# Sums of squares from the untransposed input, and the first two units of a layer with their high-part passes ahead

## The chip, the cores and the metric

The kernel runs on one core of a Trainium2 chip. The metric is the device time of one execution in microseconds. TensorE, VectorE, ScalarE and GpSimd (POOL in the profile) run their own instruction streams and wait for each other by semaphores; SyncE (SP) issues most of the DMAs.

## What is computed

The reference is a trunk of two layers over 512 tokens of width 1024, all in float32. Cut to what matters here:

```python
def rms_norm(x, g, eps=NORM_EPS):
    x32 = x.astype(F32)
    y = x32 * lax.rsqrt(jnp.mean(x32 * x32, axis=-1, keepdims=True) + eps)
    return (y * g.astype(F32)).astype(x.dtype)

for l in range(DEPTH):
    h = rms_norm(x, mix_norm_g[l])
    p_gdn, p_mla, p_rwkv, p_dsa, p_gate = _split(h @ w_in[l], SLAB_SPLITS)
    ...
    x = x + merged @ w_o[l]
    hm = rms_norm(x, mlp_norm_g[l])
    x = x + jnp.square(jax.nn.relu(hm @ w_up[l])) @ w_down[l]
return rms_norm(x, final_norm_g)
```

## The kernel before, in words

Activations are kept transposed: xT holds x as 8 tiles of 128 features by 512 tokens. The input x arrives with tokens on the partitions (`xin`, 4 tiles of 128 tokens by 1024 features, in two DMAs that each bring 512 feature columns). TensorE transposes it, one bank of 128x512 for each of the 8 feature tiles (L741, four transposes each), and VectorE copies each bank into xT (L1539).

The weights come as a stream of units; each is 1024x128 (8 blocks of 128x128, 512 KB) and goes to a ring of 3 slots. For each unit ScalarE rounds the weights to their high part (`split_next`, L1070, `w_hi`), GpSimd subtracts it to get the low part (L428, two halves, `w_lo`). The two `w_hi`/`w_lo` slots are used in turn. ScalarE's queue holds `split_next` at fixed places: units 0 and 1 at its start, each later unit just after the bank of the unit two earlier has been taken. A product of a unit with the activations is three passes of 8 matmuls into one bank (`feat_group`, `split_product`): high weights by high activations (L467) and high weights by low activations (L468) in turn, tile by tile, then low weights by high activations (L471). The pools of banks are `bank_a` (3 banks, emptied by ScalarE) and `bank_v` (4 banks, emptied by VectorE).

The norm ahead of a layer: for each tile of xT ScalarE squares it (L1078, `square`), VectorE adds it to a running 128x512 sum (L1388, `add_square`). Then TensorE sums that over the partitions with 4 matmuls against a column of ones (L494, `token_root`), which puts the sum of each token on the token's own partition: 128x4. VectorE scales it and takes the reciprocal (L1394, L1396), ScalarE the square root (L1082), and TensorE spreads it over the partitions with 4 matmuls (L500). VectorE then multiplies each tile of xT by the gain and the root (L1402, `mg`), ScalarE rounds it to its high part (L1086, `h_hi`), and VectorE subtracts to get the low part (L1406, `h_lo`). In `norm` VectorE's order is: product of tile k, then low part of tile k-1. The first unit of a layer, `("rw", 0)`, waits on TensorE for the low part of tile k before its two matmuls of that tile. It and the following ones (`project_rw(4)`) are taken from their banks by ScalarE (L1142, `take_rw`), each followed by the split of the next unit.

In layer 0 alone, VectorE computes arguments of rotary tables right after the norm (L1552 to L1568). ScalarE's queue holds two pairs of sines for them (L1134, L1135) after `h_hi` and before the first `take_rw`, with a wait for VectorE's arguments ahead of each.

Of the kernel before, what the change touches and what calls it, by code (L numbers as in the profile page):

```python
# [25 lines left out]
L = 2  # L26
# [134 lines left out]
def build(nc, x_in, pos_in, wstream, par_in, const_in, tabs, x_dram, out):  # L161
    ctx = ExitStack()
    with ctx:
# [117 lines left out]
        def at(l, name, k):  # L281

            return l * per[key[name]] + before[name] + k
# [164 lines left out]
        def _(pe):  # L448
# [38 lines left out]

            def token_root(l):

                b, reader, emptied = banks.next("v", "n_var")  # L490
                pe.wait_ge(reader, emptied)
                pe.wait_ge(S["n_acc"], at(l, "n_acc", 7))
                for t in range(TT):
                    ins = mm(b[:, t:t + 1], sums[0][:, t * P:(t + 1) * P], cst("ones")[:, 0:1], start=True, stop=True)  # L494
                ins.then_inc(v_full, 1)
                b, reader, emptied = banks.next("v", "n_g", at(l, "n_g", KT))
                pe.wait_ge(reader, emptied)
                pe.wait_ge(S["n_rs"], at(l, "n_rs", 1))
                for t in range(TT):
                    ins = mm(b[:, t * P:(t + 1) * P], root[:, t:t + 1].to_broadcast([P, P]), cst("ident"), start=True, stop=True)  # L500
                ins.then_inc(v_full, 1)
# [241 lines left out]

            for l in range(L):
                token_root(l)
                if l == 0:
# [4 lines left out]
                def project_rw(count):  # L751
                    for _ in range(count):
                        i = next(rw)
                        if i == 0:
                            feat_group(("rw", i), l, h_hi, h_lo, "a", "r_in", "n_h", at(l, "n_h", 0))
                        else:
                            feat_group(("rw", i), l, h_hi, h_lo, "a", "r_in")

# [5 lines left out]

                project_rw(4)

# [188 lines left out]
                for q in range(QUARTERS + 1):  # L955
# [7 lines left out]
                    if q >= 1:  # L963
                        for i in range(8):
# [3 lines left out]
                            else:  # L968
                                feat_group(("down", q - 1, i), l, hi, lo, "v", "down_done")
            token_root(L)  # L970
            for half in range(2):
# [11 lines left out]
        def _(act):  # L983
# [133 lines left out]
            def sums_done(name, n):  # L1117

                sums_counts[name] = sums_counts.get(name, 0) + n
                return sums_counts[name]  # L1120

            split_next()
            split_next()
            for l in range(L):
                if l == 0:
                    for k in range(KT):
                        act.wait_ge(S["x_t"], k + 1)
                        square(0, 0, k)
                norm_root(l)
# [225 lines left out]
        def _(dve):  # L1355
# [35 lines left out]
            def norm(l, gain, parts=True):  # L1391
                dve.wait_ge(v_full, filled.next())
                b = filled.bank()
                v.tensor_scalar(root, b[:, 0:TT], 1.0 / D, EPS, MUL, ADD).then_inc(S["n_var"], 1)  # L1394
                dve.wait_ge(S["n_var"], reached("n_var"))
# [3 lines left out]
                b = filled.bank()  # L1399
                for k in range(KT + 1):  # L1400
                    if k < KT:
                        ins = v.scalar_tensor_tensor(mg[:, k, :], xT[:, k, :], pr(gain, k), b[:], MUL, MUL)  # L1402
                        ins.then_inc(S["n_g"], 1)
                    if parts and k >= 1:
                        dve.wait_ge(S["n_hi"], at(l, "n_hi", k))
                        v.tensor_tensor(h_lo[:, k - 1, :], mg[:, k - 1, :], h_hi[:, k - 1, :].bitcast(F32), SUB).then_inc(S["n_h"], 1)  # L1406

# [128 lines left out]
            for k in range(KT):  # L1536
# [3 lines left out]
                dve.wait_ge(S["x_t"], reached("x_t"))  # L1540
                if k:
                    add_square(0, 0, k - 1)
            add_square(0, 0, KT - 1)

# [437 lines left out]
```

## Time and profile before

| | us |
|---|---|
| median of 3 runs | 2219.42 |
| lowest and highest run | 2217.23, 2220.02 |
| profiled execution, its time | 2219.2 |
| its span, first to last instruction | 2217.4 |
| TensorE matmul busy | 2110.0 (95%) |
| VectorE busy | 1133.7 (51%) |
| ScalarE busy | 751.1 (34%) |
| GpSimd busy | 738.3 (33%) |
| mean granted TensorE clock | 0.978 |

The profile is of one execution. Busy time of TensorE is modelled and overlaps from one matmul to the next; the distance between two starts says more. The granted clock is given as a share of 2.4 GHz. The idle time of an engine stands in brackets behind an instruction, with what ended it.

### The profile page before, as it was taken

What the parts mean: (1) busy time and instruction counts of PE and PEld (TensorE: products, weight loads), DVE (VectorE), ACT (ScalarE), POOL (GpSimd) and SP (SyncE); (2) the same over time, 40 slices, a digit from 0 to 9 for tenths busy, and PEclk for the clock granted to TensorE, in tenths of its full rate; (3) what the DMA queues carried; (4) which work ended last, traced back from release to release, by engine and by line L of the source; (5) the groups of instructions that cost most, each with busy time, mean ns of one, the idle gap of its engine ahead of it and who ended that gap; (6) DMA issues with size and microseconds to landing.
All of it is one profiled execution on the core that took longest, in us unless ns stands there. A gap on an engine that the chain in (4) does not pass through costs nothing.

```text
span 2217.4 us, 34596 instructions
## 1 busy us (share of the span) xinstructions
PE 2110.0 (95%) x14488; PEld 1630.3 (74%) x14488; DVE 1133.7 (51%) x1894; ACT 751.1 (34%) x1136; POOL 738.3 (33%) x550
## 2 busy tenths in 40 slices
PE   4999999998999999999989999999899999999997
PEld 3778787765666888888867877876565678888886
DVE  5785654897373422222256854569855534222223
ACT  3541513323342342322244253133243433322312
POOL 1540312321223444444435122133122244444442
PEclk7999999999999999999989999999899999999998
DMA  4320111221311332332232111022112123333321
GB/s 163 103 86 17 46 31 58 88 69 39 107 46 62 103 97 94 100 93 96 93 104 88 48 35 54 31 74 79 60 58 86 38 84 95 95 96 95 97 93 67
DMA packets 52266, 170.03 MB, mean 77 GB/s; under 512 B 5648, under 2 KB 13968, under 8 KB 51600
## 3 DMA queue, kind: packets, MB, share of 16 engines
q1 hardware_dynamic: 50928, 162.75, 22.8%
q0 software_dynamic: 1184, 5.07, 0.6%
q8 instruction: 116, 1.90, 0.4%
q14 instruction: 38, 0.31, 0.0%
HBM read 160.45 MB, written 7.34 MB: 76 GB/s over the span
## 4 chain that ended last, share of the span: by engine, by line
PE 77%; DVE 18%; ACT 3%; issue 2%; DMA 1%; SPq 0%; DVEq 0%; ACTq 0%
PE bank_a L467 11%; PE bank_a L468 11%; PE bank_a L471 10%; PE bank_v L471 7%; PE bank_v L467 7%; PE bank_v L468 7%; PE bank_v L607 5%; PE bank_v L529 3%; DVE arena L1776 3%; DVE m L1774 2%; PE bank_v L723 2%; PE bank_v L705 1%; DVE arena L1372 1%; DVE mg L1378 1%; DVE arena L1767 1%
## 5 line engine op out<-in xcount | busy, mean ns | idle before, releaser
L428 POOL TENSOR_TENSOR w_lo<-ring,w_hi 128x512 fp32r<-128x512 f32 x536 | 731.8, 1386 | 1309.7 <-ACT w_hi L1070 1309.6
L467 PE MATMUL bank_a<-h_hi,w_hi 128*128 128x512 f32 x1376 | 561.2, 408 | 8.2 <-DVE h_lo L1406 4.8
L468 PE MATMUL bank_a<-h_lo,w_hi 128*128 128x512 f32 x1376 | 540.9, 393 | 0.0
L1070 ACT ACTIVATE w_hi<-ring 128x1024 fp32r<-128x1024 f32 x268 | 281.6, 1051 | 234.5 <-DVE arena L1881 220.2
L471 PE MATMUL bank_a<-h_hi,w_lo 128*128 128x512 f32 x1376 | 340.0, 389 | 0.0
L467 PEld LDWEIGHTS bank_a<-h_hi,w_hi 128*128 128x128 f32 x1376 | 260.7, 189 | 86.4 <-issue 18.8
L468 PEld LDWEIGHTS bank_a<-h_lo,w_hi 128*128 128x128 f32 x1376 | 261.5, 190 | 60.9 <-issue 8.7
L471 PEld LDWEIGHTS bank_a<-h_hi,w_lo 128*128 128x128 f32 x1376 | 258.4, 188 | 53.9
L1372 DVE TENSOR_TENSOR sg<-bank_v,sg 128x512 f32<-128x512 f32 x112 | 77.5, 692 | 349.4 <-PE bank_v L471 256.5
L467 PE MATMUL bank_v<-parts,w_hi 128*128 128x512 f32 x640 | 254.4, 398 | 1.4 <-DVE parts L1852 1.4
L468 PE MATMUL bank_v<-parts,w_hi 128*128 128x512 f32 x640 | 253.4, 396 | 0.0
L1871 DVE TENSOR_TENSOR arena<-arena 128x512 f32<-128x512 f32 x64 | 44.3, 692 | 245.2 <-ACT arena L1336 245.1
L471 PE MATMUL bank_v<-parts,w_lo 128*128 128x512 f32 x640 | 162.2, 395 | 0.0
L467 PEld LDWEIGHTS bank_v<-parts,w_hi 128*128 128x128 f32 x640 | 120.3, 188 | 32.7 <-DVE parts L1852 4.0
L468 PEld LDWEIGHTS bank_v<-parts,w_hi 128*128 128x128 f32 x640 | 120.1, 188 | 29.5 <-issue 0.5
L471 PEld LDWEIGHTS bank_v<-parts,w_lo 128*128 128x128 f32 x640 | 120.2, 188 | 29.1
L607 PE MATMUL bank_v<-arena 64*64 64x64 f32 x3712 | 112.1, 219 | 5.9 <-DVE arena L1447 5.0
L607 PEld LDWEIGHTS bank_v<-arena 64*64 64x64 f32 x3712 | 110.7, 135 | 7.0 <-DVE arena L1447 5.7
L529 PE MATMUL bank_v<-yo,out_ring 128*128 128x512 f32 x256 | 114.0, 592 | 0.0
L1336 ACT ACTIVATE arena<-bank_a 128x512 f32<-128x512 f32 x64 | 38.3, 598 | 205.6 <-PE bank_a L471 205.6
L1372 DVE TENSOR_TENSOR arena<-arena 128x512 f32<-128x512 f32 (+5 forms) x80 | 88.1, 1102 | 37.7 <-ACT arena L1142 29.4
L1040 ACT ACTIVATE sg<-bank_a 128x512 f32<-128x512 f32 x56 | 33.4, 597 | 212.4 <-PE bank_a L471 212.4
(267 smaller groups left out, 2441.7 us busy)
## 6 DMA issues: line engine op xcount, KB each, us to landing
ring<-in_w SPq DMA_DIRECT2D x268, 512.0 KB, 3.5
out_ring<-in_w SPq DMA_DIRECT2D x64, 128.0 KB, 3.5
x_dram<-arena SPq DMA_DIRECT2D x2, 2048.0 KB, 7.6
arena<-x_dram SPq DMA_DIRECT2D x2, 2048.0 KB, 8.1
arena<-in_x SPq DMA_DIRECT2D x2, 1024.0 KB, 8.6
arena<-tabs POOLq DMA_DIRECT2D x4, 512.0 KB, 4.0
out_x<-arena SPq DMA_DIRECT2D x2, 1024.0 KB, 4.4
par<-in_par POOLq DMA_DIRECT2D x2, 937.0 KB, 7.0
```

Source lines behind the costliest of these rows:

```text
L428: ins = nc.gpsimd.tensor_tensor(w_lo[:, g % SPLIT, ks, :], raw, w_hi[:, g % SPLIT, ks, :].bitcast(F32), ALU.subtract)
L467: mm(b[:], w_hi[:, s, k, :], hi[:, k, :], start=k == 0, stop=False)
L468: mm(b[:], w_hi[:, s, k, :], lo[:, k, :], start=False, stop=False)
L471: ins = mm(b[:], w_lo[:, s, k, :], hi[:, k, :], start=False, stop=k == KT - 1)
L529: ins = mm(b[:], out_ring[:, n % OUT_RING, k, :], yo[:, slot, k, :], start=k == 0, stop=k == 1)
L607: ins = mm(b[quarter(p_), k * C:(k + 1) * C], lhs[quarter(p_), m, :], rhs(m, p_), start=True, stop=True)
L723: ins = mm(b[rows, 0:P], v[:, k, h * C:(h + 1) * C], V_pt(x)[:, j % 2, k, :], start=k == 0, stop=k == qt)
L1070: act_fn(w_hi[:, g % SPLIT, :, :], ring[:, g % RING, :, :], ACT.Copy).then_inc(S["split_hi"], 1)
L1372: link(v.tensor_tensor(out_, a, b, op))
L1774: link(v.max(m8[:], src))
L1776: link(v.match_replace(wk, m8[:], src, -3e38))
L1871: v.tensor_tensor(relu2[:, n % 2, :], relu[:, n % 2, :], relu[:, n % 2, :], MUL).then_inc(S["up_sq"], 1)
```

## The change

Three things are changed. In layer 0, ScalarE squares `xin` itself, 8 pieces of 128 tokens by 512 features, with a sum along the row (`accum_out`) into 8 columns of `att`; it does so before the splits of units 0 and 1. VectorE adds the two halves (128x4) into `root`. The squares of xT, their sums and the 4 matmuls of L494 are gone in layer 0; in layer 1 and in the final norm they stay (`token_sums`). In `norm`, VectorE issues all 8 products and then all 8 low parts. On TensorE, `project_first` takes the place of the first two of `project_rw(4)`, in both layers: for unit 0 and then unit 1, tile by tile, high by high and low weights by high activations; then the 8 low-activation matmuls of unit 0, then those of unit 1.

```diff
@@ -485,7 +485,7 @@
                 pe.wait_ge(S["n_acc"], at(l, "n_acc", 14))
                 mm(b[:], cst("ones"), sums[1], start=True, stop=True).then_inc(v_full, 1)
 
-            def token_root(l):
+            def token_sums(l):
 
                 b, reader, emptied = banks.next("v", "n_var")
                 pe.wait_ge(reader, emptied)
@@ -493,6 +493,9 @@
                 for t in range(TT):
                     ins = mm(b[:, t:t + 1], sums[0][:, t * P:(t + 1) * P], cst("ones")[:, 0:1], start=True, stop=True)
                 ins.then_inc(v_full, 1)
+
+            def token_root(l):
+
                 b, reader, emptied = banks.next("v", "n_g", at(l, "n_g", KT))
                 pe.wait_ge(reader, emptied)
                 pe.wait_ge(S["n_rs"], at(l, "n_rs", 1))
@@ -742,6 +745,10 @@
                 ins.then_inc(v_full, 1)
 
             for l in range(L):
+                if l == 0:
+                    banks.counts["n_var"] = 1
+                else:
+                    token_sums(l)
                 token_root(l)
                 if l == 0:
                     pe.wait_ge(more_here, 16)
@@ -750,11 +757,26 @@
 
                 def project_rw(count):
                     for _ in range(count):
-                        i = next(rw)
-                        if i == 0:
-                            feat_group(("rw", i), l, h_hi, h_lo, "a", "r_in", "n_h", at(l, "n_h", 0))
-                        else:
-                            feat_group(("rw", i), l, h_hi, h_lo, "a", "r_in")
+                        feat_group(("rw", next(rw)), l, h_hi, h_lo, "a", "r_in")
+
+                def project_first():
+
+                    open_ = []
+                    for _ in range(2):
+                        g = begin_unit(("rw", next(rw)), l)
+                        b, reader, emptied = banks.next("a", "r_in")
+                        pe.wait_ge(reader, emptied)
+                        pe.wait_ge(S["split_lo"], g + 1)
+                        open_.append((g % SPLIT, b))
+                        for k in range(KT):
+                            pe.wait_ge(S["n_hi"], at(l, "n_hi", k + 1))
+                            mm(b[:], w_hi[:, g % SPLIT, k, :], h_hi[:, k, :], start=k == 0, stop=False)
+                            mm(b[:], w_lo[:, g % SPLIT, k, :], h_hi[:, k, :], start=False, stop=False)
+                    for s, b in open_:
+                        for k in range(KT):
+                            pe.wait_ge(S["n_h"], at(l, "n_h", k + 1))
+                            ins = mm(b[:], w_hi[:, s, k, :], h_lo[:, k, :], start=False, stop=k == KT - 1)
+                        ins.then_inc(a_full, 1)
 
                 def low_rank(weights, act_tile):
                     for f in range(2):
@@ -762,7 +784,8 @@
                         pe.wait_ge(reader, emptied)
                         mm(b[:], weights[:, f * P:(f + 1) * P], act_tile, start=True, stop=True).then_inc(a_full, 1)
 
-                project_rw(4)
+                project_first()
+                project_rw(2)
 
                 pe.wait_ge(S["r_act"], at(l, "r_act", 1))
                 low_rank(pr("wa2")[0:64, :], R["rm"][0:64, 6, :])
@@ -967,6 +990,7 @@
                                 feat_group(("down", q - 1, i), l, hi, lo, "v", "down_done", "up_done", at(l, "up_done", 8 * (q - 1)))
                             else:
                                 feat_group(("down", q - 1, i), l, hi, lo, "v", "down_done")
+            token_sums(L)
             token_root(L)
             for half in range(2):
                 for t in range(TT):
@@ -1119,13 +1143,14 @@
                 sums_counts[name] = sums_counts.get(name, 0) + n
                 return sums_counts[name]
 
+            for half in range(2):
+                act.wait_ge(x_here[half], 16)
+                for t in range(TT):
+                    act_fn(ar(8 + TT * half + t, (T,)), xin[:, t, half * T:(half + 1) * T], ACT.Square,
+                           accum_out=att[:, half, t:t + 1]).then_inc(S["n_sq"], 1)
             split_next()
             split_next()
             for l in range(L):
-                if l == 0:
-                    for k in range(KT):
-                        act.wait_ge(S["x_t"], k + 1)
-                        square(0, 0, k)
                 norm_root(l)
                 if l == 0:
 
@@ -1389,21 +1414,21 @@
                     dve.wait_ge(S["n_acc"], reached("n_acc"))
 
             def norm(l, gain, parts=True):
-                dve.wait_ge(v_full, filled.next())
-                b = filled.bank()
-                v.tensor_scalar(root, b[:, 0:TT], 1.0 / D, EPS, MUL, ADD).then_inc(S["n_var"], 1)
+                token_sum = root
+                if l:
+                    dve.wait_ge(v_full, filled.next())
+                    token_sum = filled.bank()[:, 0:TT]
+                v.tensor_scalar(root, token_sum, 1.0 / D, EPS, MUL, ADD).then_inc(S["n_var"], 1)
                 dve.wait_ge(S["n_var"], reached("n_var"))
                 v.reciprocal(root, root).then_inc(S["n_rec"], 1)
                 dve.wait_ge(S["n_rec"], reached("n_rec"))
                 dve.wait_ge(v_full, filled.next())
                 b = filled.bank()
-                for k in range(KT + 1):
-                    if k < KT:
-                        ins = v.scalar_tensor_tensor(mg[:, k, :], xT[:, k, :], pr(gain, k), b[:], MUL, MUL)
-                        ins.then_inc(S["n_g"], 1)
-                    if parts and k >= 1:
-                        dve.wait_ge(S["n_hi"], at(l, "n_hi", k))
-                        v.tensor_tensor(h_lo[:, k - 1, :], mg[:, k - 1, :], h_hi[:, k - 1, :].bitcast(F32), SUB).then_inc(S["n_h"], 1)
+                for k in range(KT):
+                    v.scalar_tensor_tensor(mg[:, k, :], xT[:, k, :], pr(gain, k), b[:], MUL, MUL).then_inc(S["n_g"], 1)
+                for k in range(KT if parts else 0):
+                    dve.wait_ge(S["n_hi"], at(l, "n_hi", k + 1))
+                    v.tensor_tensor(h_lo[:, k, :], mg[:, k, :], h_hi[:, k, :].bitcast(F32), SUB).then_inc(S["n_h"], 1)
 
             def low_part(l, k):
 
@@ -1538,9 +1563,10 @@
                 b = filled.bank()
                 v.tensor_copy(xT[:, k, :], b[:]).then_inc(S["x_t"], 1)
                 dve.wait_ge(S["x_t"], reached("x_t"))
-                if k:
-                    add_square(0, 0, k - 1)
-            add_square(0, 0, KT - 1)
+            dve.wait_ge(S["n_sq"], 8)
+            v.tensor_tensor(root, att[:, 0, :], att[:, 1, :], ADD).then_inc(S["n_acc"], 7)
+            counts["n_acc"] = 7
+            dve.wait_ge(S["n_acc"], 7)
 
             for l in range(L):
                 dve.wait_ge(par_here, 16 * (l + 1))
```

ScalarE's queue at the start, before. L1078 are the squares of xT, L1082 the root:

```order
L1070 ACT_TABLE_LOAD
L1070 ACTIVATE w_hi<-ring 128x1024 x2
L1078 ACTIVATE arena<-arena 128x512 x8
L1082 ACT_TABLE_LOAD
L1082 ACTIVATE sml<-sml 128x4
L1086 ACTIVATE h_hi<-mg 128x512 x8
```

And with the change, where L1149 are the squares of `xin`, L1094 the splits and L1106 the root:

```order
L1149 ACT_TABLE_LOAD
L1149 ACTIVATE arena,att<-arena 128x512 x8
L1094 ACTIVATE w_hi<-ring 128x1024 x2
L1106 ACT_TABLE_LOAD
L1106 ACTIVATE sml<-sml 128x4
L1110 ACTIVATE h_hi<-mg 128x512 x8
```

The squares moved ahead of the two splits, and nothing but a table load now stands between splits and root.

VectorE in the start and norm of layer 0, before (the pair of L1402 and L1406 goes on to 8 each):

```order
L1539 COPY arena<-bank_v3 128x512
L1388 TENSOR_TENSOR arena<-arena 128x512 x2
L1394 TENSOR_SCALAR sml<-bank_v0 128x4
L1396 RECIPROCAL sml<-sml 128x4
L1402 SCALAR_TENSOR_TENSOR mg<-arena,par,bank_v1 128x512 x2
L1406 TENSOR_TENSOR h_lo<-mg,h_hi 128x512
L1402 SCALAR_TENSOR_TENSOR mg<-arena,par,bank_v1 128x512
```

And with the change:

```order
L1564 COPY arena<-bank_v3 128x512
L1567 TENSOR_TENSOR sml<-att 128x4
L1421 TENSOR_SCALAR sml<-sml 128x4
L1423 RECIPROCAL sml<-sml 128x4
L1428 SCALAR_TENSOR_TENSOR mg<-arena,par,bank_v0 128x512 x8
L1431 TENSOR_TENSOR h_lo<-mg,h_hi 128x512 x8
L1578 CAST arena<-arena 128x512
```

The large sums (L1388) are gone, and products and low parts stand in two blocks ahead of the tables' first instruction.

TensorE in the first two units, before:

```order
L500 MATMUL bank_v1<-consts,sml 128x128 x4
L467 MATMUL bank_a0<-h_hi,w_hi 128x512
L468 MATMUL bank_a0<-h_lo,w_hi 128x512
...
L471 MATMUL bank_a0<-h_hi,w_lo 128x512 x8
L467 MATMUL bank_a1<-h_hi,w_hi 128x512
```

And with the change:

```order
L503 MATMUL bank_v0<-consts,sml 128x128 x4
L773 MATMUL bank_a0<-h_hi,w_hi 128x512
L774 MATMUL bank_a0<-h_hi,w_lo 128x512
...
L773 MATMUL bank_a1<-h_hi,w_hi 128x512
L774 MATMUL bank_a1<-h_hi,w_lo 128x512
...
L778 MATMUL bank_a0<-h_lo,w_hi 128x512 x8
L778 MATMUL bank_a1<-h_lo,w_hi 128x512 x8
```

All 16 matmuls that read low activations moved behind the 32 that read high ones; unit 0's bank is complete 8 matmuls before unit 1's.

## Rows read from the trace of the kernel before

**Rows 1.** The page, chain that ended last, by engine.

```profile
PE 77%; DVE 18%; ACT 3%; issue 2%; DMA 1%; SPq 0%; DVEq 0%; ACTq 0%
```

**Rows 2.** Timeline, start of layer 0: start us, us, engine, line, operation [idle before].

```profile
8.69 4.57 PE L741 MATMUL bank_v<-consts,arena 128*128 128x128 f32 x24 [8.69 <-DMA arena<-in_x]
9.91 1.51 DVE L1539 COPY arena<-bank_v 128x512 f32<-128x512 f32 x2 [7.32 <-PE bank_v L741]
16.11 1.06 ACT L1070 ACTIVATE w_hi<-ring 128x1024 fp32r<-128x1024 f32 x1 [14.09 <-DMA ring<-in_w]
17.25 5.39 POOL L428 TENSOR_TENSOR w_lo<-ring,w_hi 128x512 fp32r<-128x512 f32 x4 [15.30 <-ACT w_hi L1070]
17.39 1.06 ACT L1070 ACTIVATE w_hi<-ring 128x1024 fp32r<-128x1024 f32 x1 [0.22 <-DMA ring<-in_w]
...
19.05 0.69 DVE L1539 COPY arena<-bank_v 128x512 f32<-128x512 f32 x1 [7.63 <-ACT arena L1078]
...
28.95 1.28 ACT L1082 ACT_TABLE_LOAD   x1
...
32.26 0.20 ACT L1082 ACTIVATE sml<-sml 128x4 f32<-128x4 f32 x1 [2.03 <-DVE sml L1396]
...
34.77 1.41 DVE L1402 SCALAR_TENSOR_TENSOR mg<-arena,par,bank_v 128x512 f32<-128x512 f32 x2 [2.54 <-PE bank_v L500]
```

**Rows 3.** Timeline of the norm in layer 0, and last line the final norm.

```profile
39.34 0.74 DVE L1402 SCALAR_TENSOR_TENSOR mg<-arena,par,bank_v 128x512 f32<-128x512 f32 x1
...
40.11 0.63 ACT L1086 ACTIVATE h_hi<-mg 128x512 fp32r<-128x512 f32 x1 [0.63 <-DVE mg L1402]
40.60 0.74 DVE L1402 SCALAR_TENSOR_TENSOR mg<-arena,par,bank_v 128x512 f32<-128x512 f32 x1
...
44.55 0.69 DVE L1406 TENSOR_TENSOR h_lo<-mg,h_hi 128x512 fp32r<-128x512 f32 x1
...
2202.88 5.36 DVE L1402 SCALAR_TENSOR_TENSOR mg<-arena,par,bank_v 128x512 f32<-128x512 f32 x8 [2.54 <-PE bank_v L500]
```

**Rows 4.** Timeline, the sine that waits in layer 0 and unit 2's first matmul.

```profile
53.78 0.63 ACT L1134 ACTIVATE arena<-arena 128x512 f32<-128x512 f32 x1 [2.93 <-DVE arena L1562]
...
56.42 0.59 PE L467 MATMUL bank_a<-h_hi,w_hi 128*128 128x512 f32 x1 [2.56 <-ACT w_hi L1070]
```

**Rows 5.** Timeline, layer 1: the norm's start, units 0 and 1 taken.

```profile
1120.70 1.41 DVE L1402 SCALAR_TENSOR_TENSOR mg<-arena,par,bank_v 128x512 f32<-128x512 f32 x2 [2.54 <-PE bank_v L500]
...
1134.18 0.60 ACT L1142 ACTIVATE arena<-bank_a 128x512 f32<-128x512 f32 x1 [3.73 <-PE bank_a L471]
...
1139.62 0.60 ACT L1142 ACTIVATE arena<-bank_a 128x512 f32<-128x512 f32 x1 [3.89 <-PE bank_a L471]
```

**Rows 6.** Windows: stretch, us, busy PE, PEld, DVE, ACT, POOL, granted clock, DMA share, GB/s.

```profile
37.00:46.00 9.00, 8.76 (x16) 4.12 (x17) 8.87 (x15) 5.07 (x7) 0.00 (x0) 0.50 0.00 0
...
56.40:60.00 3.60, 3.58 (x9) 2.84 (x10) 3.50 (x3) 1.40 (x2) 3.56 (x3) 0.54 0.00 0
1122.00:1131.00 9.00, 7.82 (x13) 3.51 (x14) 8.87 (x15) 4.52 (x8) 0.00 (x0) 0.50 0.58 245
```

**Rows 7.** Groups by line with shapes: an ACTIVATE that sums along the row.

```profile
L1095 ACT ACTIVATION_READ_ACCUMULATOR arena<-arena,att 128x1 f32 x64 | 12.0, 187 | 0.0
...
L1095 ACT ACTIVATE arena<-arena,att 128x512 f32<-128x512 f32 x16 | 11.6, 723 | 21.3 <-DVE att L1512 21.3
```

**Rows 8.** Timeline, a table load and the ACTIVATE behind it.

```profile
65.33 1.28 ACT L1159 ACT_TABLE_LOAD   x1
...
66.62 0.63 ACT L1159 ACTIVATE arena<-arena 64x512 f32<-64x512 f32 x1
```

**Rows 9.** Timeline, matmuls in unit 2 of layer 0, and 8 at full clock.

```profile
57.66 0.63 PE L468 MATMUL bank_a<-h_lo,w_hi 128*128 128x512 f32 x1
...
58.08 0.63 PE L467 MATMUL bank_a<-h_hi,w_hi 128*128 128x512 f32 x1
...
1137.61 1.98 PE L471 MATMUL bank_a<-h_hi,w_lo 128*128 128x512 f32 x8
```

## The prediction

> **What bounds the kernel now.** I read three views in this order. First the chain that ended last: TensorE is 77% of it, VectorE 18% [rows 1]. So time is won only where TensorE stands still or runs at its lower clock while others work, and the change touches two such places: the start of each layer. Then the timeline: the first 57 us [rows 2, 3, 4], the same place in layer 1 [rows 5]. Last the granted clock by stretch [rows 6].
>
> At the start of layer 0 TensorE transposes x from 8.69. VectorE empties two banks, and its next copy begins at 19.05, with 7.63 us of waiting for ScalarE's first square [rows 2]. ScalarE stood in its queue at the two weight splits, which waited for DMA until 16.11 and 17.39 and end at 17.39 + 1.06 = 18.45. Only then do the squares and their sums start, alternating between ScalarE and VectorE until the table load at 28.95. The gain multiplication, which I call the norm's start S, comes at 34.77 [rows 2].
>
> After S each of the 8 tiles costs 1.26 us (39.34 to 40.60), because VectorE alternates product and low part and the product waits behind the low part of the tile before [rows 3]. The last low part ends at 44.55 + 0.69 = 45.24, that is S + 10.47. TensorE follows tile by tile and is granted 0.50 of full speed, the 1.2 GHz level, all through it [rows 6]. VectorE then computes arguments of the rotary tables. ScalarE waits for them with the first unit's bank and the split of unit 2 behind them in its queue. So unit 2's first matmul is at 56.42, after 2.56 us in which TensorE had nothing to do [rows 4]. Layer 1 has no tables there: unit 0 is taken at 1134.18 and unit 1 at 1139.62, so unit 1 was done about 18.9 us after its S of 1120.70 [rows 5].
>
> **The change, part by part.**
>
> *Squares from x as it arrives.* Removed: 8 squares and 7 VectorE sums, 4 matmuls (L494) in layer 0. Added: 8 squares on ScalarE that also sum along the row, and one 128x4 addition. Such an ACTIVATE of 128x512 takes 723 ns and its READ_ACCUMULATOR 187 ns [rows 7], so 0.91 us each. Four may start when the first half of x is there (8.69), until 12.3. The second half was there before TensorE ended its 24 transposes at 13.26 [rows 2], since six column tiles need it. Four more end between 16.0 and 16.9. The two splits stand behind them, but could not start before 16.11 anyway, and the second not before 17.39. So they end at 18.45 or up to 0.5 later. I take 18.5.
>
> VectorE now copies eight banks back to back: 1.51 us for two [rows 2], so 9.91 + 8 x 0.75 = 15.9. The addition and two small operations end before 16.7, or 17.6 with late squares. So the root waits only for ScalarE: 18.5, table load 1.28 = 19.8, root 0.20 = 20.0. From the root's end (32.26 + 0.20 = 32.46) to S it took 2.31 us [rows 2]. New S: 22.3, that is **12.5 us earlier** (12.0 to 12.5).
>
> The load's price is weighed here. A load of 1.28 us at 65.33 is followed by its ACTIVATE at 66.62 [rows 8], so nothing more than the load is on the path. The Trainium skill, page "ScalarE: Activation LUTs", section "What ACT_TABLE_LOAD costs", adds about 1.38 us of drain to every switch, 2.66 us together. By the page S would be 23.7 and the gain of this part 11.1; [rows 8] decide, and the sum goes by them.
>
> *POOL's queue and DMA.* GpSimd makes the low parts of units 0 and 1 from 17.25 to 22.64 [rows 2]. Unit 0 is ready halfway, at 20.0, before the new S, and unit 1 at 22.6, long before TensorE asks. The copy of xT to DRAM is issued some 5 us earlier, behind the same two ring loads; nobody waits for it until much later. Cost nothing.
>
> *VectorE's order within the norm.* Eight products back to back took 5.36 us in the final norm [rows 3], 0.66 apart. The eight low parts follow at 0.62 to 0.73 apart (a row of 0.69, less an overlap like that of the products, or with a step between them). The last ends at S + 10.2 to 11.1, and I take S + 10.5, as before. So the rotary tables start as before relative to S and **unit 2 still starts 21.65 us after S**: about 44.0 in place of 56.42. In layer 0 the new order of units 0 and 1 gains nothing, for TensorE will be done by about 38 and then idles some 6 us. That wait hides the whole of it. Were the tables gone, it would be worth what layer 1 shows.
>
> *Low clock behind that wait.* After the wait of 2.56 us the granted clock is 0.54 from 56.4 to 60.0 [rows 6]. Matmuls were 0.42 us apart there (57.66, 58.08), against (1.98 - 0.39) / 7 = 0.227 at full clock [rows 9]. Eight matmuls cost 8 x 0.19 = 1.6 us more. A longer wait leads to the same half clock. I take the same 1.6 us, so 0 change. Bounds: 1.6 gained if the clock is back at once, 2.6 lost if it takes the 9 us that the paced start took.
>
> *TensorE's order, layer 1.* The high part of tile k is ready at S + 0.77 + 0.63 + 0.66 k [rows 3], so TensorE starts at S + 1.45 and no longer waits for low parts. It has 16 + 16 high-part matmuls, then 8 + 8 low-part ones. Before, 16 matmuls were spread over 10 us. Now two per tile take 0.85 us at the lower clock against a supply of 0.66, so TensorE is fed without gaps. The open size is when the clock rises. As nearest rows, the unbroken unit 2 of layer 0 had it back 3.6 us after its first matmul; the paced starts had 0.50 for 9 us [rows 6].
> - Back after 3.6 us: 8.5 matmuls by S + 5.1. The supply then paces until S + 6.5, and the other 32 take 32 x 0.227 = 7.3: end S + 13.8, gain 5.1.
> - Back after 9 us: 21 matmuls by S + 10.5, 27 more in 6.1: end S + 16.6, gain 2.3.
>
> I take 5 us, nearer to the unbroken row: 11.8 matmuls by S + 6.5, 36.2 x 0.227 = 8.2, end S + 14.7, **gain 4.2**. Low parts are in time: the last is at S + 10.5, needed after S + 12. Unit 2's split is now behind unit 0's late end: taking the bank and splitting are 0.5 + 1.05 us, and unit 0 ends 8 matmuls = 1.8 us before unit 1. So this new wait stays covered, by 0.2 us.
>
> *Final norm*: same work. **Sum**: 12.5 - 0.1 + 4.2 = 16.6, of which I keep 16.4 for small handovers. The profiled execution took 2219.2 (span 2217.4), so 2202.8; the median of the runs is 0.2 higher, so **2203.0 us**.
>
> **The rivals.**
> 1. *The clock gives less.* Layer 1 keeps 0.50 for 9 us, and the longer wait before unit 2 costs 2.6 more: 12.4 + 2.3 - 2.6 = 12.1, 2207. For it: [rows 6], two paced starts of 9 us. Against it: these had gaps, the new one has none.
> 2. *ScalarE's queue moves late.* Each us by which the squares end after 16.1 pushes both splits, root and S. For a gain below 10.5 they would need 0.7 us more each than the rows of such squares show [rows 7]. Also a piece of the 12.4 could vanish in a later wait for another engine. Some 6 us of gain left: 2213.
> 3. *The change does not do what it says*: the norm's start in layer 0 still waits for an input that I see as landed, and the layer 1 order is worth nothing as unit 2's split is late: 2218.
> 4. *Slower: the half clock spreads.* Place: layer 0, from the new wait before unit 2 on, and layer 1's first units. Each us of unbroken matmuls at 1.2 GHz costs 1 - 0.227/0.42 = 0.46 us. To lose 16.4 and another 4.4 (0.2%), 45 us more at 0.50 are needed. The trace shows 9 us at most in one piece [rows 6]. If all 48 matmuls of both first pairs stayed low, layer 1 would end at S + 1.45 + 20.2 = 21.6, 2.7 us later than before, still far from it. From 45 us on it decides: 2224.
>
> **How the numbers follow.** 0.2% of this time, 4.4 us, is about what a measurement of this kernel can tell from no change. Forecast 0.71 (its own range 2199 to 2206: 5.1 in place of 4.2, a clock 1.6 better, and the same down). Rival 1 has 0.17, rival 2 0.07, rival 3 0.03, rival 4 0.02. Forecast, rival 1 and rival 2 are faster by more than 4.4: 0.95, less 0.01 for rival 2's tail. Rival 3 and that tail are the same: 0.04. Slower 0.02. The range 2198.5 to 2209 holds the forecast and rival 1 with its bound.
>
> **What would show it.** In the new profile: eight copies without a gap until 16, splits at 16.1 and 17.4, gain products from 22.3, table arguments from 33, unit 2's first matmul at 44.0 with 5 to 7 us of idle time before it, released by the split; in layer 1 matmuls from S + 1.45 without gaps and unit 1 taken at S + 14.7, last low part at S + 10.5. Wrong are the steps where S falls later than 23, where unit 2 begins later than 45.5, or where layer 1's unit 1 is taken after S + 17. A span that moves less than these three together would speak for a later wait.

## The result and the profile after

The changed kernel took 2201.57 us (median of 4 runs, 2198.79 to 2202.93) against 2219.18 (4 runs, 2217.23 to 2220.02): ratio 0.992, 95% interval 0.9903 to 0.9937, 17.6 us less. The profiled execution took 2201.45 us with a span of 2199.7.

Where the 17.7 us of the span came from, at five places of the two timelines:

| place | before | after | earlier by |
|---|---|---|---|
| S, layer 0 | 34.77 | 22.32 | 12.45 |
| unit 2's first matmul, layer 0 | 56.42 | 43.68 | 12.74 |
| S, layer 1 | 1120.70 | 1108.98 | 11.72 |
| unit 1 taken, layer 1 | 1139.62 | 1123.44 | 16.18 |
| S, final norm | 2202.88 | 2185.13 | 17.75 |

The timeline of the changed kernel at the start answers to [rows 2]. Columns: start us, us, engine, line, operation, [idle before]:

```profile
8.76 0.63 ACT L1149 ACTIVATE arena<-arena 128x512 f32<-128x512 f32 x1 [6.73 <-DMA arena<-in_x]
...
13.89 0.19 ACT L1149 ACTIVATION_READ_ACCUMULATOR arena<-arena 128x1 f32 x1
...
16.16 1.06 ACT L1094 ACTIVATE w_hi<-ring 128x1024 fp32r<-128x1024 f32 x1 [2.09 <-DMA ring<-in_w]
...
17.44 1.06 ACT L1094 ACTIVATE w_hi<-ring 128x1024 fp32r<-128x1024 f32 x1 [0.22 <-DMA ring<-in_w]
18.52 1.28 ACT L1106 ACT_TABLE_LOAD   x1
19.81 0.21 ACT L1106 ACTIVATE sml<-sml 128x4 f32<-128x4 f32 x1
20.16 2.05 PE L503 MATMUL bank_v<-consts,sml 128*128 128x128 f32 x8 [6.25 <-ACT sml L1106]
22.32 5.36 DVE L1428 SCALAR_TENSOR_TENSOR mg<-arena,par,bank_v 128x512 f32<-128x512 f32 x8 [5.61 <-PE bank_v L503]
```

The eight squares run from 8.76 to 14.08 and are over 2 us before the first split can start. The root follows the table load at once. TensorE's start and unit 2, which answer to [rows 3, 4]:

```profile
23.88 0.77 PE L773 MATMUL bank_a<-h_hi,w_hi 128*128 128x512 f32 x1 [1.67 <-ACT h_hi L1110]
...
27.59 4.91 DVE L1431 TENSOR_TENSOR h_lo<-mg,h_hi 128x512 fp32r<-128x512 f32 x8
...
33.51 3.79 PE L778 MATMUL bank_a<-h_lo,w_hi 128*128 128x512 f32 x16
...
43.68 0.80 PE L467 MATMUL bank_a<-h_hi,w_hi 128*128 128x512 f32 x1 [6.38 <-ACT w_hi L1094]
```

TensorE has done both units at 37.3 and then waits 6.38 us for the split behind the sines; before it was 2.56. The windows view, with the columns of [rows 6], shows what follows:

```profile
23.80:28.40 4.60, 4.52 (x11) 3.60 (x12) 4.60 (x8) 4.43 (x8) 0.00 (x0) 0.50 0.93 364
28.40:37.30 8.90, 8.90 (x39) 6.99 (x37) 8.62 (x16) 1.58 (x2) 0.00 (x0) 0.98 0.23 96
37.30:43.60 6.30, 0.00 (x1) 0.00 (x0) 5.81 (x12) 3.37 (x7) 0.00 (x0) 0.90 0.01 1
43.60:49.00 5.40, 5.32 (x13) 4.17 (x14) 5.24 (x5) 1.46 (x3) 5.30 (x4) 0.50 0.25 66
1110.50:1114.00 3.50, 3.46 (x8) 2.80 (x9) 3.50 (x6) 3.37 (x6) 0.00 (x0) 0.50 1.03 430
1114.00:1121.00 7.00, 7.00 (x32) 5.70 (x31) 5.34 (x11) 0.99 (x2) 0.00 (x0) 0.99 0.25 105
```

Fed without gaps, TensorE was at full clock 4.9 us after its first matmul in layer 0 and 3.6 us after it in layer 1, where the paced starts of [rows 6] had 0.50 for 9 us. But behind the long wait it had 0.50 from 43.6 to 49.0, which is why 12.74 us shrank to 11.75 when unit 2's bank was taken (63.77 before, 52.02 after). In layer 1, answering to [rows 5]:

```profile
1121.62 0.60 ACT L1167 ACTIVATE arena<-bank_a 128x512 f32<-128x512 f32 x1 [6.61 <-PE bank_a L778]
...
1123.44 0.60 ACT L1167 ACTIVATE arena<-bank_a 128x512 f32<-128x512 f32 x1 [0.27 <-PE bank_a L778]
```

Unit 1 is taken 14.46 us after S, where it was 18.92.

### The profile page after: what moved, and what is told of

It reads as the page before. It is cut to its first block, busy times and chain, and to the rows that moved or that the text cites. A ratio compares the mean times of both kernels' runs of the same rounds, so it can differ in the third digit from the quotient of the medians.

```text
span 2199.7 us, 34572 instructions
## 1 busy us (share of the span) xinstructions
PE 2100.2 (95%) x14480; PEld 1627.7 (74%) x14480; DVE 1127.3 (51%) x1888; ACT 752.1 (34%) x1144; POOL 739.9 (34%) x550
## 4 chain that ended last, share of the span: by engine, by line
PE 77%; DVE 18%; ACT 3%; issue 1%; DMA 1%; SPq 0%; DVEq 0%; ACTq 0%
PE bank_a L467 11%; PE bank_a L468 10%; PE bank_a L471 10%; PE bank_v L471 7%; PE bank_v L467 7%; PE bank_v L468 7%; PE bank_v L610 5%; PE bank_v L532 3%; DVE arena L1802 3%; DVE m L1800 3%; PE bank_v L726 2%; PE bank_v L708 1%; DVE arena L1397 1%; DVE mg L1403 1%; DVE arena L1793 1%
## 5 line engine op out<-in xcount | busy, mean ns | idle before, releaser
L467 PE MATMUL bank_a<-h_hi,w_hi 128*128 128x512 f32 x1344 | 543.5, 404 | 6.8 <-ACT w_hi L1094 6.8
L468 PE MATMUL bank_a<-h_lo,w_hi 128*128 128x512 f32 x1344 | 525.3, 391 | 0.0
L1094 ACT ACTIVATE w_hi<-ring 128x1024 fp32r<-128x1024 f32 x268 | 281.7, 1051 | 222.4 <-DVE arena L1907 220.1
L471 PE MATMUL bank_a<-h_hi,w_lo 128*128 128x512 f32 x1344 | 332.0, 389 | 0.0
L467 PEld LDWEIGHTS bank_a<-h_hi,w_hi 128*128 128x128 f32 x1344 | 253.5, 189 | 75.1 <-issue 13.5
L468 PEld LDWEIGHTS bank_a<-h_lo,w_hi 128*128 128x128 f32 x1344 | 253.6, 189 | 60.4 <-issue 8.7
L471 PEld LDWEIGHTS bank_a<-h_hi,w_lo 128*128 128x128 f32 x1344 | 252.3, 188 | 52.4
```

The lines of the kernel that those rows point to most:

```text
L467: mm(b[:], w_hi[:, s, k, :], hi[:, k, :], start=k == 0, stop=False)
L468: mm(b[:], w_hi[:, s, k, :], lo[:, k, :], start=False, stop=False)
L471: ins = mm(b[:], w_lo[:, s, k, :], hi[:, k, :], start=False, stop=k == KT - 1)
L1094: act_fn(w_hi[:, g % SPLIT, :, :], ring[:, g % RING, :, :], ACT.Copy).then_inc(S["split_hi"], 1)
```

## The experiments

Eleven kernels ran, each timed against the kernel before on the same chip. The median of the kernel before was 2218.59 us beside e1 to e4, 2218.89 beside e5, e6, e7 and e9, and 2218.66 beside e10 to e12. S, "unit 2" and "unit 1 taken" are the places of the table above; all line numbers in rows are those of the kernel named.

### Taking the change apart

**e1_squares**: the early squares alone.

```diff
-                project_first()
-                project_rw(2)
+                project_rw(4)
...
-                for k in range(KT):
-                    v.scalar_tensor_tensor(mg[:, k, :], xT[:, k, :], pr(gain, k), b[:], MUL, MUL).then_inc(S["n_g"], 1)
-                for k in range(KT if parts else 0):
+                for k in range(KT + 1):
```

> Only the squares from the untransposed x; norm order and TensorE's order of units 0 and 1 as before. Theory (the early start is worth 12.4 us in layer 0, and the new order is worth nothing there because the rotary tables hold unit 2 back; it is worth 4.5 us in layer 1 alone): S of layer 0 at 22.3, unit 2's first matmul at 43.7 to 44.0, layer 1's unit 1 taken at its S + 18.9, total 2206.5 us. Rival (the order gives 4 us in both layers): unit 2 only at 47.5 and total about 2210. Either may be off by 1.6 us for each piece of 3.4 us at the lower clock more or less.

Measured: 2205.93 us (2205.05 to 2206.22), ratio 0.9943 (0.9926 to 0.9959). S at 22.45, unit 2 at 44.12, unit 1 of layer 1 taken at S + 19.00. The theory held and the rival, with unit 2 at 47.5, falls.

**e2_order**: both new orders, the squares as before. The diff is against the kernel before; those of the other runs are against the changed kernel.

```diff
-                project_rw(4)
+                project_first()
+                project_rw(2)
...
-                for k in range(KT + 1):
...
+                for k in range(KT):
+                    v.scalar_tensor_tensor(mg[:, k, :], xT[:, k, :], pr(gain, k), b[:], MUL, MUL).then_inc(S["n_g"], 1)
+                for k in range(KT if parts else 0):
```

> Only the new orders on VectorE and TensorE, in both layers; the squares as before. Theory: unit 2 of layer 0 at 56.4 as before, since it is released by ScalarE after the tables; unit 1 of layer 1 at S + 14.5 in place of 18.9; total 2214.7 us. Rival (the order gives 4 us in both layers): unit 2 at 52.5, total 2210.

Measured: 2213.39 us (10 runs, 2211.34 to 2217.09), ratio 0.9977 (0.9968 to 0.9987). Unit 2 at 56.15, after a wait of 6.97 us; unit 1 of layer 1 taken at S + 14.12. So the early squares are worth 12.7 us and the orders 5.2, and 17.9 is the whole change within the spread. In layer 0 the orders did not move unit 2 (56.42 to 56.15).

**e3_pe_old** and **e4_alt**: the changed kernel with one of the two orders put back.

```diff
-                project_first()
-                project_rw(2)
+                project_rw(4)
```

> The changed kernel with TensorE's old order of units 0 and 1; VectorE's eight products stay ahead of the eight low parts. Theory (the gain of layer 1 needs both orders): the first matmul waits for the first low part, at S + 6.0 in place of S + 1.5, then unit 1 ends at about S + 18.6, as before the change; total 2206 us. Rival (VectorE's order alone does it): S + 15, total 2201.6.

```diff
-                for k in range(KT):
-                    v.scalar_tensor_tensor(mg[:, k, :], xT[:, k, :], pr(gain, k), b[:], MUL, MUL).then_inc(S["n_g"], 1)
-                for k in range(KT if parts else 0):
+                for k in range(KT + 1):
```

> The changed kernel with VectorE's old order, product and low part in turn; TensorE's new order stays. Theory: high parts come 1.26 us apart, so the high passes of unit 0 last until S + 10.5 with gaps, the clock stays at 0.50 until about then, and unit 1 ends at S + 18 to 19.5; total 2206 us. Rival (TensorE's order alone does it): S + 15, total 2201.6.

Measured: 2205.21 us (2202.98 to 2205.87) and 2203.81 (2202.49 to 2207.24). Layer 1's unit 1 was taken at S + 19.62 and S + 18.46. Both rivals fall: against the S + 19.00 of e1_squares, one order without the other is 0.6 us later or 0.5 earlier in layer 1, where both together are 4.5 earlier. The timeline of e3_pe_old shows the new wait that VectorE's blocks make for TensorE's old order:

```profile
1105.20 5.36 DVE L1431 SCALAR_TENSOR_TENSOR mg<-arena,par,bank_v 128x512 f32<-128x512 f32 x8 [2.54 <-PE bank_v L503]
1110.47 4.90 DVE L1434 TENSOR_TENSOR h_lo<-mg,h_hi 128x512 fp32r<-128x512 f32 x8
...
1111.31 0.77 PE L467 MATMUL bank_a<-h_hi,w_hi 128*128 128x512 f32 x1 [6.21 <-DVE h_lo L1434]
```

One number was not expected: e3_pe_old has its S of layer 1 at 1105.20, where the changed kernel has 1108.98. In layer 0 its unit 2 began at 43.84 after a wait of only 1.46 us, and its bank was taken at 49.62, in the changed kernel at 52.02. That raised a question that the prediction had not: does TensorE's new order cost something in layer 0?

### What the place of the squares and of the root is worth

**e9_late**: the squares behind the two splits.

```diff
+            split_next()
+            split_next()
             for half in range(2):
                 act.wait_ge(x_here[half], 16)
...
-            split_next()
-            split_next()
```

> The changed kernel with the eight squares behind the two weight splits on ScalarE. Theory: squares from 18.5, 0.62 us apart as in the changed kernel's trace, until 23.5, S at 27.3 in place of 22.3, unit 2 at 48.7, total 2206.6 us. Rival (the place of the squares does not matter, as the splits and DMA set S): S at 22.5, total 2201.6.

Measured: 2205.8 us (2203.7 to 2207.38). S at 27.33 and unit 2 at 48.68, 5.0 us later than in the changed kernel; the median is 4.2 above. The rival falls. S is still 7.4 us earlier than in the kernel before, so of the 12.45 us the place in the queue gave 5.0. The other 7.4 came with the squares of `xin` themselves, which need no turns with VectorE's copies and sums and no matmuls of L494.

**e7_root**: the root ahead of the splits, its inputs computed between two of VectorE's copies.

```diff
                 act_fn(root, root, ACT.Sqrt).then_inc(S["n_rs"], 1)
+                if l == 0:
+                    split_next()
+                    split_next()
...
-            split_next()
-            split_next()
...
             for k in range(KT):
+                if k == 6:
+                    dve.wait_ge(S["n_sq"], 8)
+                    v.tensor_tensor(root, att[:, 0, :], att[:, 1, :], ADD).then_inc(S["n_acc"], 7)
...
                 v.tensor_copy(xT[:, k, :], b[:]).then_inc(S["x_t"], 1)
```

> The changed kernel, with the root of layer 0 ahead of the two weight splits on ScalarE, and the addition and reciprocal between VectorE's sixth and seventh copy. Theory (the splits, which wait for the weights' DMA, and the table load behind them set S): S at 17.9 in place of 22.3, unit 2 at 39.3, total 2197.2 us. Rival (the norm now runs beside GpSimd's low parts, 17.3 to 22.6, and its products are slowed): S at 17.9 but the last low part less than 2 us earlier than in the changed kernel, total 2200.

Measured: 2195.18 us (2194.64 to 2195.92), ratio 0.9894 (0.9879 to 0.9909), 6.4 below the changed kernel. Its timeline:

```profile
15.23 0.20 ACT L1106 ACTIVATE sml<-sml 128x4 f32<-128x4 f32 x1
...
15.58 1.13 PE L503 MATMUL bank_v<-consts,sml 128*128 128x128 f32 x8 [1.52 <-ACT sml L1106]
16.01 1.06 ACT L1094 ACTIVATE w_hi<-ring 128x1024 fp32r<-128x1024 f32 x1 [0.58 <-DMA ring<-in_w]
16.85 5.36 DVE L1427 SCALAR_TENSOR_TENSOR mg<-arena,par,bank_v 128x512 f32<-128x512 f32 x8 [0.71 <-PE bank_v L503]
17.16 5.00 POOL L428 TENSOR_TENSOR w_lo<-ring,w_hi 128x512 fp32r<-128x512 f32 x4 [15.19 <-ACT w_hi L1094]
```

S is 5.47 us earlier and unit 2 5.48 (38.20). I had expected 4.4: TensorE's spreading matmuls (L503) take 1.13 us in place of 2.05, for they come 1.52 us behind the transposes and have a granted clock of 1.00 (15.5 to 16.8), where in the changed kernel they come after 6.25 us and have 0.50 (20.1 to 22.3). The eight products beside GpSimd's low parts take 5.36 us, as without them, and the last low part of the norm ends 5.5 us earlier, so that rival falls.

### Whether the tables are the whole bound of layer 0

**e5_tables**: ScalarE takes units 0 and 1, and splits units 2 and 3, ahead of the sines.

```diff
-                if l == 0:
-
-                    for i in range(2):
-                        act.wait_ge(S["tab_arg"], i + 1)
...
-                for i in range(3):
-                    take_rw(i)
+                take_rw(0)
+                take_rw(1)
+                if l == 0:
+
+                    for i in range(2):
+                        act.wait_ge(S["tab_arg"], i + 1)
...
+                take_rw(2)
```

> The changed kernel, with ScalarE taking units 0 and 1 and splitting units 2 and 3 ahead of the sines in layer 0. Theory (the tables alone hold unit 2 back, and the low clock behind the wait is a cost of that wait): unit 2's first matmul at about 37.5 in place of 43.7 with almost no idle time, no fall of the clock there, 8.8 us less up to there; some of it given back before the low-rank matmuls, since VectorE still has the tables to do, slowed while GpSimd splits units 2 and 3: total 2194.5 us (2192 to 2197). Rival (VectorE is the bound of that stage whatever ScalarE does): all given back at the low-rank matmuls, total 2200 to 2202.

Measured: 2201.86 us (2201.52 to 2202.58). The rival's total was right: all was given back, though not where it had said.

```profile
34.18 2.14 DVE L1404 SCALAR_TENSOR_TENSOR arena<-arena 128x512 f32<-128x512 f32 x3
...
37.65 6.12 POOL L428 TENSOR_TENSOR w_lo<-ring,w_hi 128x512 fp32r<-128x512 f32 x4 [15.55 <-ACT w_hi L1094]
39.26 5.06 DVE L1404 SCALAR_TENSOR_TENSOR arena<-arena 128x512 f32<-128x512 f32 x3
...
48.33 3.33 DVE L1607 SCALAR_TENSOR_TENSOR arena<-arena,par 128x512 f32<-128x512 f32 x1
...
51.73 1.28 ACT L1185 ACT_TABLE_LOAD   x1 [4.33 <-DVE arena L1607]
...
53.71 6.20 PE L785 MATMUL bank_a<-arena,par 64*128 64x512 f32 x8 [4.92 <-ACT arena L1185]
```

TensorE went on to unit 2 at 37.6, but the low-rank matmuls (L785) wait 4.92 us for ScalarE, and that 4.33 us for VectorE. VectorE was busy for 28.5 of the 29.4 us from S on: three operations of the second table took 5.06 us beside GpSimd's splits, where the first table's took 2.14, and the operation that ScalarE waits for (L1607) took 3.33 us, the next one like it 0.75. So VectorE's work is the bound up to there, not only the place of the split in ScalarE's queue. Yet the low-rank matmuls still begin 3.65 us earlier than in the changed kernel (57.36). The rest was given back behind them, by the clock. First e5_tables, then the changed kernel:

```profile
53.80:64.00 10.20, 10.20 (x18) 5.39 (x19) 8.48 (x20) 5.75 (x8) 3.09 (x2) 0.50 0.19 59
```

```profile
57.30:64.00 6.70, 6.40 (x23) 3.91 (x23) 5.66 (x7) 4.13 (x7) 3.12 (x2) 1.00 0.37 101
```

Behind its 4.92 us of waiting e5_tables has half clock for 10.2 us, some 4.7 us lost at the prediction's 0.46 for each (an estimate). At layer 1's S it is 1.66 us behind the changed kernel (1110.64).

**e6_tables_pe_old**: the same with TensorE's old order.

```diff
-                project_first()
-                project_rw(2)
+                project_rw(4)
```

> As the run with the sines moved behind units 0 and 1, but with TensorE's old order of units 0 and 1. Theory (the new order is worth about 4 us wherever nothing hides it): unit 2 of layer 0 at about 41 in place of 37.5, layer 1's unit 1 at S + 18.6; total about 8 us above the run with the new order, 2202. Rival (the order is worth something only in layer 1): unit 2 at 37.5, total 4 us above.

Measured: 2208.64 us (2207.89 to 2209.57), 6.8 above e5_tables, where 8 and 4 stood against each other. Unit 2's first matmul is at 42.19 against 37.64, so with nothing in its way the order is worth 4.5 us in layer 0 too, and the rival's 37.5 falls. But the low-rank matmuls begin at 55.38 in place of 53.71, and of these 1.7 us 0.6 are left at layer 1's S (1111.24 against 1110.64). The rest comes in layer 1: unit 1 is taken at S + 19.67 against S + 14.22, and from S to the final S it takes 6.4 us longer.

**e11_rotor**: the first table's arguments moved into VectorE's wait for the root.

```diff
                 v.reciprocal(root, root).then_inc(S["n_rec"], 1)
                 dve.wait_ge(S["n_rec"], reached("n_rec"))
+                if l == 0:
+                    dve.wait_ge(more_here, 16)
+                    dve.wait_ge(pos_here, 16)
+                    link(v.tensor_copy(POS["f"], POS["i"]))
+                    arguments(0, rotors[0])
...
-                    for i, nm in enumerate(rotors):
...
+                    arguments(1, rotors[1])
```

> The changed kernel, with the arguments of the first rotary table moved on VectorE to where it waits for the root in layer 0 (16.7 to 22.3). Theory (VectorE's work after the norm holds unit 2 back, but beside GpSimd's low parts the same work takes about 8 us in place of 4.1): S late at 24.5, unit 2 at about 41.5, total 2199 us. Rival (the wait for the root covers it all): S at 22.3, unit 2 at 39.6, total 2197. Rival (it only moves work about): total 2201.6.

Measured: 2197.5 us (2195.06 to 2199.66). S fell later than expected, to 25.79, as that piece took 8.4 us beside GpSimd's low parts, and unit 2 came at 42.59, only 1.1 us earlier. Yet the time is 4.1 lower. TensorE waited 2.43 us ahead of unit 2 in place of 6.38, had full clock behind it, and unit 2's bank was taken at 48.37, 3.65 us earlier; S of layer 1 is at 1105.35, still 3.6 earlier. The theory's price for the piece (about 8 us) held, but S and unit 2 came 1.3 and 1.1 us later than it said, and its total was met only with the help of the clock behind unit 2, which it did not have. The rivals' S of 22.3 falls.

### Whether TensorE's new order costs in layer 0

**e10_l1_only**: the changed kernel, with the new order in layer 1 alone.

```diff
-                project_first()
-                project_rw(2)
+                if l:
+                    project_first()
+                    project_rw(2)
+                else:
+                    project_rw(4)
```

> The changed kernel, with TensorE's new order of units 0 and 1 in layer 1 alone; layer 0 has the old one behind VectorE's blocks. Theory (in layer 0 the new order wins nothing and makes TensorE wait longer ahead of unit 2, after which the clock is low; the run with the old order in both layers reached layer 1's S at 1105.2, the changed kernel at 1109.0): S of layer 1 at 1105.2, the rest as in the changed kernel, total 2197.8 us. Rival (the difference at layer 1's S was chance of the clock): S at 1107 to 1109, total 2201.6.

Measured: 2199.46 us (2197.54 to 2200.97), ratio 0.9912 (0.9897 to 0.9926). S of layer 1 at 1105.74. Its windows, to be held against 43.60:49.00 above:

```profile
28.70:41.30 12.60, 12.58 (x48) 10.01 (x48) 12.12 (x22) 2.39 (x3) 0.00 (x0) 0.87 0.16 68
43.90:49.00 5.10, 5.03 (x22) 4.18 (x23) 4.98 (x4) 1.46 (x3) 5.00 (x4) 1.00 0.20 55
```

TensorE starts unit 0 at 28.72 instead of 23.88 and runs without gaps until 41.3, waits 2.63 us, and does unit 2 at full clock: 22 matmuls in 5.1 us where the changed kernel has 13 in 5.4. In this execution the later start cost 0.3 us at unit 2 (43.97) and kept the clock. S of layer 1 speaks against the rival; the median, halfway between 2197.8 and 2201.6, does not decide.

**e12_root_l1**: the root of e7_root and the layer choice of e10_l1_only together.

```diff
-                project_first()
-                project_rw(2)
+                if l:
+                    project_first()
+                    project_rw(2)
+                else:
+                    project_rw(4)
```

> The root ahead of the two splits, and TensorE's new order in layer 1 alone. Theory (both gains add, since one moves S and the other what follows unit 2): S of layer 0 at 16.9, unit 2 at 38.2 with 1.5 us of idle time before it, S of layer 1 at 1099.7, total 2192 us. Rival (the second gain is gone, as TensorE waits for GpSimd's low part of unit 0 or the clock falls otherwise): 2195.5.

Measured: 2193.21 us (2192.18 to 2196.0), ratio 0.9886 (0.9871 to 0.9901), the fastest of all: 25.5 us under the kernel before. Unit 2 at 38.68 after 2.17 us, S of layer 1 at 1101.54. The total is nearer to the theory's 2192 than to the rival's 2195.5, though S of layer 1 is 1.8 us later than it said.

The changes of TensorE's order in layer 0 are small beside the spread: 2.1 us for e10_l1_only against the changed kernel, 2.0 for e12_root_l1 against e7_root, with ranges that meet. All profiled executions together say more (e5 and e6 have another ScalarE queue there and are left out). From unit 2's first matmul until its bank was taken it took 5.8 us in e3, e10, e11 and e12, where the granted clock stayed at 1.00. It took 7.2 to 7.4 in the kernel before, e1, e4 and e9, 7.8 in e2 and 8.3 in the changed kernel and e7, where it fell to 0.50. From unit 2's first matmul to layer 1's S the four that kept the clock took 1062.2 us on average (1061.4 to 1062.9), the seven that lost it 1064.6 (1063.5 to 1065.6).

The length of the wait alone does not tell which of the two comes. The kernel before and e1 waited 2.56 and 2.75 us and lost the clock, e10 waited 2.63 and kept it. This is e1:

```profile
32.20:41.40 9.20, 9.16 (x36) 7.12 (x36) 8.68 (x16) 2.45 (x4) 0.00 (x0) 0.92 0.01 2
44.10:47.40 3.30, 3.28 (x8) 2.61 (x9) 3.23 (x3) 1.39 (x2) 3.26 (x3) 0.50 0.00 0
```

What differs ahead of the wait is that e1 and the kernel before had run without a gap for 9.2 and 9.3 us, behind paced matmuls, and e10 for 12.6. Whether that is the cause was not tried. One execution of each kernel is traced, and those of e3 and e10 were the fastest of their four, by 2.1 and 1.9 us, so that their others need not have kept the clock. That all five that waited 3.8 us or longer lost it is what the traces show for the new order in layer 0.

## Why the prediction was right, point by point

The forecast was 2203.0, measured 2201.57; its steps held as follows.

- **S at 22.3**: 22.32, gain 12.45 of 12.5. Inside it a term was too large: a square with its sum cost 0.62 us, not 0.91. The ACTIVATE took 0.62 where the row of [rows 7] had 0.72, and the READ_ACCUMULATOR of 0.19 lies beside the end of its ACTIVATE and the start of the next. The slack ahead of the splits hid the error, as [rows 2] had promised: the splits wait for DMA in both kernels. e9_late shows what the place in the queue is worth of this, 5.0 us.
- **The table load**: the 1.28 us of [rows 8] held. Load at 18.52, root at 19.81. The extra 1.38 us of drain that the Trainium skill gives in "ScalarE: Activation LUTs", section "What ACT_TABLE_LOAD costs", did not show here either; S would have been at 23.7.
- **VectorE's blocks**: products 5.36 us as in [rows 3], low parts 4.91, 0.60 apart (expected 0.62 to 0.73). The last ends at S + 10.2. Unit 2 therefore came 21.36 us after S, not 21.65.
- **The new order wins nothing in layer 0**: e2_order shows it for unit 2. The step "the clock behind the longer wait costs the same" was wrong in size. The clock was back 5.5 us after unit 2's first matmul in place of 3.7, and the 12.74 us at unit 2's start were 11.75 when its bank was taken: 1.0 us lost, inside the bound of 2.6. Against e10, which kept the clock, 2.6 are lost at that place. Not hidden and harmless, as I had it, but slightly harmful.
- **Layer 1**: 4.2 expected, 4.46 measured up to unit 1. The clock was back after 3.6 us, as in the unbroken row, and not after my 5. By the prediction's bound for 3.6 us the gain should then have been 5.1, but that bound has a slip. It lets the supply pace TensorE until S + 6.5 and counts 16 matmuls by then, where 8.5 by S + 5.1 and 1.4 us at 0.227 make 14.7. TensorE was never paced; 39.5 x 0.227 behind S + 5.1 end at S + 14.1, gain 4.8. It began at S + 1.56, not 1.45, and ended at S + 14.4. The new wait for unit 2's split was not covered: the bank of unit 2 was taken 5.55 us after unit 1's, where 24 matmuls take 5.44. That is 0.1 us.
- **The half clock in one piece**: rival 4's "9 us at most in one piece" is a misreading. [rows 6] are cuts of 9 us out of longer stretches; in the kernel before the clock is 0.50 from 1118.3 to 1131.8, with TensorE busy for 10.7 of the 13.5 us. The 45 us that the rival needs are far off even so.
- **The total**: it came within 1.4 us partly by luck. Measured against the 16.4, 1.0 us was lost behind unit 2, where the sum had 0, and more than won back by 0.3 at unit 2's start, 0.3 in layer 1's first units, 0.3 taken off for small handovers that did not come, and the next point.
- **Mis-sized**: what layer 1 is worth as a whole. From its S to the final S it took 1075.9 us on average in the eight kernels with both new orders in layer 1 (1075.2 to 1077.8) and 1081.8 in the five without (1081.3 to 1082.2), so 5.9 us. The missing 1.5 lies far behind the change. The kernel before has a stretch of low clock with TensorE busy there, and the changed kernel, at the same place about 17 us earlier, has none. First the kernel before, then the changed one:

```profile
1554.00:1562.00 8.00, 8.00 (x23) 4.83 (x24) 6.64 (x11) 2.98 (x5) 0.00 (x0) 0.79 0.15 58
```

```profile
461.00:467.00 6.00, 5.95 (x13) 3.15 (x14) 4.66 (x8) 2.99 (x5) 0.00 (x0) 0.72 0.23 83
...
1540.00:1570.00 30.00, 30.00 (x116) 21.43 (x114) 28.60 (x56) 9.46 (x13) 9.19 (x8) 1.00 0.13 42
```

  e1, e4 and e6 have this stretch in layer 1 too. e3, with TensorE's old order, has not, and no kernel with both new orders has it. From unit 1 taken to the final S it takes 1062.9 us on average in the four with it and 1061.5 in the nine without. In layer 0 the changed kernel has such a stretch at 462 and the kernel before does not; there e4, e5, e6, e7, e11 and e12 have it as well and e1, e2, e3, e9 and e10 do not, so that it goes with neither order. Each is 3.4 us at 0.50, some 1.6 us lost at 0.46 for each (an estimate). What decides whether it comes was not tried and stays open; so does whether the 1.5 us belong to the change.
- **The rivals**: the clock did rise early in layer 1, so of rival 1 only the loss behind layer 0's wait came, 1.0 us of its 2.6. Rivals 2, 3 and 4 did not come; e9_late is what rival 2 would have looked like, with 5.0 of the 12.4 lost at S and 4.2 in the median.

## What to carry to other kernels

A reordering pays only up to the next wait that it does not move: behind the tables of layer 0 the same TensorE order won nothing that was worth 4.5 us in layer 1, and finishing early there only made TensorE's pause 6.38 us long, with half clock for the 5.5 us behind it. e5_tables shows the same behind a pause of 4.92 us: a wait can cost more than its length, through the slow matmuls after it. When an engine's queue holds instructions that wait for a DMA, ask what stands behind them and need not: taking the squares past the weight splits won 5.0 us of the 12.45 at S (e9_late), and taking the root past them 5.5 more (e7_root). And moving a wait out of one queue (e5_tables) shows whether that queue or the engine behind it was the bound.

## What the runs showed of the hardware

- Eight squares with a sum along the row took 5.3 us, 0.62 apart, though ACTIVATE and READ_ACCUMULATOR last 0.61 to 0.63 and 0.19: the READ_ACCUMULATOR (9.90 to 10.09) starts before its ACTIVATE ends (9.99), and ends after the next has started (10.00).
- TensorE at half clock rose to full after 3.6 and 4.9 us of matmuls without gaps in the changed kernel, but not in 9 us of paced ones that were busy by the modelled count for 8.76 of 9.0 us [rows 6].
- Waits of nearly one length ended in either clock: 1.00 behind 2.63 us (e10), 0.50 for some 3.4 us behind 2.56 (the kernel before) and 2.75 (e1). Behind 3.85 to 6.97 us it fell to 0.50 in all five traces (the changed kernel, e2, e4, e7, e9).
- In e5_tables, VectorE operations that read two SBUF tiles took over twice as long beside GpSimd's subtraction (5.06 us for three against 2.14). In e11_rotor, TENSOR_SCALARs that read one SBUF tile and write one slowed as well (2.77 us for two, 0.89 in the changed kernel). In e7_root, products with one SBUF tile and one bank took the same as alone (5.36 us for eight).
